# Thirty-two bytes ahead of the arena: every tile of the attention and FFN stages starts on another address

## The reference: what is computed

```
x = even_layer(rms_norm(x)) + x      # sliding-window attention beside an S5 state-space mixer
x = odd_layer(rms_norm(x)) + x       # attention to the 128 keys that an index picks per query
for layer in 0, 1:                   # second block
    h = h + merge_heads(concat(mix, memory)) @ w_out[layer]   # forget-gate attention, then dilated attention
    h = h + conv_ffn(rmsnorm(h))                              # below
return rmsnorm(h, norm_final)

def conv_ffn(xn, w_up, conv_w, conv_b, w_down):
    u = xn @ w_up                    # 512x1024 @ 1024x5632
    c = conv_b + sum(conv_w[j] * shifted(u, j) for j in range(3))
    val, gate = split(c)
    return (silu(gate) * val) @ w_down   # 512x2816 @ 2816x1024
```

## Time and profile before

| | us |
|---|---|
| median of 3 runs | 1809.51 |
| lowest and highest run | 1806.91, 1810.58 |
| the profiled execution's own time | 1806.99 |
| span of its trace | 1805.2 |
| its mean granted TensorE clock | 0.994 of 2.4 GHz |

### The profile page before, as it was taken

One profiled execution on the slowest core, in us unless ns is written; L12 is line 12 of the kernel. 1 busy time (PEld: TensorE's weight loads), 2 busy tenths in 40 slices (PEclk: granted clock), 3 DMA queues, 4 the chain that ended last, 5 costly groups with the idle time before them and its releaser, 6 DMA issues.

```text
span 1805.2 us, 24432 instructions
## 1 busy us (share of the span) xinstructions
PE 1759.5 (97%) x9567; PEld 1404.3 (78%) x9572; DVE 940.4 (52%) x1896; ACT 533.6 (30%) x1183; POOL 1015.1 (56%) x1046
## 2 busy tenths in 40 slices
PE   7999999999989999999999999999999999999998
PEld 6886678676668967779888888887677888888886
DVE  5976754695543355533663166335765356415642
ACT  3614534312542344423220012023664211101111
POOL 7533375554237744335777677756434577677762
PEclk9989999999999999999999999999999999999999
DMA  5220312230233321113332333222111233233331
GB/s 177 82 77 19 117 59 94 77 99 29 71 105 106 94 71 50 69 47 90 106 98 88 95 99 104 88 94 71 49 69 48 70 94 114 96 93 94 95 103 47
DMA packets 170994, 151.16 MB, mean 84 GB/s; under 512 B 5192, under 2 KB 145992, under 8 KB 170880
## 3 DMA queue, kind: packets, MB, share of 16 engines
q1 hardware_dynamic: 169280, 148.12, 26.8%
q10 hardware_dynamic: 1600, 1.48, 0.3%
HBM read 147.45 MB, written 2.14 MB: 83 GB/s over the span
## 4 chain that ended last, share of the span: by engine, by line
PE 93%; DVE 4%; ACT 2%; issue 1%; another core or an unknown queue 0%; DMA 0%; ACTq 0%; DVEq 0%
PE ps L281 77%; PE ps L1989 3%; PE ps L2022 2%; PE ps L2007 2%; PE ps L352 1%; PE ps L640 1%; PE ps L1486 1%; PE ps L1464 1%; PE ps L1995 1%; PE ps L1407 1%; PE ps L1415 1%; PE ps L665 1%; PE ps L1423 0%; PE ps L672 0%; PE ps L1476 0%
## 5 line engine op out<-in xcount | busy, mean ns | idle before, releaser
L127 POOL TENSOR_SCALAR w_hi<-w_raw 128x512 fp32r<-128x512 f32 x520 | 315.7, 635 | 747.0 <-PE ps L281 742.3
L131 POOL TENSOR_TENSOR w_lo<-w_raw,w_hi 128x512 fp32r<-128x512 f32 x520 | 694.5, 1367 | 11.3
L281 PE MATMUL ps<-x_hi,w_hi 128*128 128x512 f32 (+1 forms) x1448 | 538.0, 372 | 0.7 <-DVE x_lo L434 0.7
L281 PE MATMUL ps<-x_hi,w_lo 128*128 128x512 f32 (+1 forms) x1448 | 527.9, 365 | 0.0
L281 PE MATMUL ps<-x_lo,w_hi 128*128 128x512 f32 (+1 forms) x1448 | 527.9, 365 | 0.0
L281 PEld LDWEIGHTS ps<-x_hi,w_hi 128*128 128x128 f32 x1448 | 274.8, 190 | 69.0 <-issue 19.8
L281 PEld LDWEIGHTS ps<-x_hi,w_lo 128*128 128x128 f32 x1448 | 274.8, 190 | 43.7
L281 PEld LDWEIGHTS ps<-x_lo,w_hi 128*128 128x128 f32 x1448 | 275.1, 190 | 40.8 <-issue 0.5
L2291 DVE SCALAR_TENSOR_TENSOR ffn_cv<-ps,col,ffn_cv 128x510 f32<-128x510 f32 (+1 forms) x176 | 131.8, 749 | 192.3 <-ACT ffn_cv L2269 187.6
L2269 ACT ACTIVATE ffn_cv<-ps,col 128x512 f32<-128x512 f32 x88 | 63.8, 775 | 500.2 <-PE ps L281 500.2
L309 DVE TENSOR_TENSOR h<-h,ps 128x512 f32<-128x512 f32 x64 | 43.9, 687 | 261.4 <-PE ps L281 261.3
(11 more groups left out here) (346 smaller groups left out, 2394.1 us busy)
## 6 DMA issues: line engine op xcount, KB each, us to landing
w_raw<-w_up SPq DMA_DIRECT2D x88, 512.0 KB, 5.0
w_raw<-w_down SPq DMA_DIRECT2D x16, 1024.0 KB, 5.0
w_raw<-od_w_in SPq DMA_DIRECT2D x12, 1024.0 KB, 5.2
w_raw<-w_in_fox SPq DMA_DIRECT2D x10, 1024.0 KB, 5.3
w_raw<-w_in_dil SPq DMA_DIRECT2D x10, 1024.0 KB, 5.1
w_raw<-w_out SPq DMA_DIRECT2D x8, 1024.0 KB, 5.0
w_raw<-ev_w_in SPq DMA_DIRECT2D x7, 1024.0 KB, 5.3
w_raw<-w_down SPq DMA_DIRECT2D x8, 768.0 KB, 4.5
```

The source lines that it names most:

```text
L127: ins = pool.tensor_scalar(hi[:, c:min(c + PIECE, size)], raw[:, c:min(c + PIECE, size)], 1.0, 1.0, ALU.mult, ALU.mult)
L131: ins = pool.tensor_tensor(lo[:, c:min(c + PIECE, size)], raw[:, c:min(c + PIECE, size)], hi[:, c:min(c + PIECE, size)].bitcast(F32), ALU. ...
L281: mm = pe.matmul(o, l, r, start=start and i == 0, stop=stop and i == 2)
```

## The change

One tensor of 32 bytes per partition, which nobody reads or writes, is allocated ahead of the arena. The arena's start goes from 133,984 to 134,016, a multiple of 64 bytes (and of 128, as the starts of the weight slots, `h`, `x_hi` and `x_lo` are). Every tile in the arena moves up by 32 bytes. No instruction is added, removed or moved on any engine, and no shape changes; only addresses do.

More of the change, by code:

```diff
@@ L1282, in block_kernel @@
         soft_stat = sb("soft_stat", [P, 4, 4])
+        sb("arena_pad", [P, -nc.sbuf_base % 64 // 4])
         sb("arena", [P, 92 * KB // 4])
```

## The result

The changed kernel takes 1800.82 us, median of 6 runs (1795.70 to 1803.19), against 1809.02 us (1806.91 to 1810.58, 6 runs) for the kernel before: a ratio of 0.9949, with a 95% interval from 0.9931 to 0.9967. That is 8.2 us less. The forecast was 10.6 us less. The profiled execution took 1799.54 us, with a span of 1797.7 us and a mean granted clock of 0.993; before, these were 1806.99 us, 1805.2 us and 0.994.

The account below looks back on a forecast made before the run. TensorE was taken to bound the kernel, through start distances of back-to-back matmuls. 10.1 (back-to-back) + 0.7 (fill) - 0.2 (memory) = 10.6 us off 1,809.51 gave 1,798.9 us, range 1,793 to 1,810 us.

Parts of the forecast that it names:

- The bound: Whole kernel: TensorE bounds, and over each FFN the chain is matmuls alone, so distances between their starts set the time.
- The back-to-back products: 1,527 products of 512 columns with an arena operand, issued without gaps: 6.6 ns less each, 10.1 us gained.
- A line of 64 bytes: Reason given for 6.6 ns per product: an operand starting off a multiple of 64 streams one 64-byte line more.
- The rival of the place: TensorE reads the upper part of a partition more slowly, so nothing changes: 1,809.5 us; 0.20 together with another no-change rival.
- The fill: 201 products between attention steps, worth 1.3 us; half taken, 0.7 us gained, with none to all in the range.
- The memory: 192 products of 256 columns there might get slower once aligned: 0.2 us taken as cost, 0 to 1.0 kept.
- Plain float32, VectorE, ScalarE: Transposes, scores, values and VectorE, ScalarE work: zero taken; reserves up to 5 us gain on transposes, 4.7 us on ScalarE.
- The total: Whole kernel: 10.6 us less, 1,798.9 us; forecast of 1,794 to 1,801 us given a chance of 0.74.

Follow-up runs that it names:

- arena_64_not_128: Changed kernel with a filler of 96 bytes: arena on 134,080, a multiple of 64 but not of 128; 1807.81 us, ratio 1.0000 to the kernel before.
- all_off32: Changed kernel with weights, h, x and arena all moved to 32 bytes past a multiple of 64 (160 modulo 256); 1798.61 us, ratio 0.9947.
- arena_plus160: Changed kernel with a filler of 160 bytes: arena on a multiple of 256, weights and x on 128 modulo 256; 1807.93 us, ratio 0.9999.
- x_off32: Changed kernel with x_hi and x_lo moved to 32 bytes past a multiple of 64, arena on a multiple of 256; 1823.08 us, ratio 1.0081.
- w_lo_off32: Changed kernel with only w_lo moved, to 160 modulo 256, all other operands and the arena on 128; 1822.29 us, ratio 1.0080.
- x_plus160: Changed kernel with x_hi and x_lo begun 160 bytes past the weights' place modulo 256, arena on that place; 1823.23 us in one execution.

## Why the prediction was right, and where it was not

**The bound** was read rightly: the chain of the FFNs shrank by what its products did, and no other engine stepped in.

**The back-to-back products.** 6.6 ns on 1,056 of them in the FFNs makes 7.0 us; the two long pieces gave 3.39 + 3.53 = 6.92 us. The mixers' output projections gave 1.0 us each. The odd output projection gave 0.3 us, where its 72 back-to-back products make 0.5. The step in the earlier trace rows was a sound measure of the gain, since it compared the same instruction with two addresses in one execution.

**The reason given for it was wrong.** "A line of 64 bytes" made the change look necessary and sufficient: any start on a multiple of 64 would do. arena_64_not_128 is on such a start and gains nothing, and all_off32 is on none and gains all. The rows ahead of the prediction showed two groups that differ in the remainder modulo 64, but they differed just as much in whether both operands have the same remainder; the weight slots, x and h are all on 128 modulo 256, so the two could not be told apart. The change happened to fit both, since 134,016 is 128 modulo 256. A filler made by the same rule in another kernel could have landed on 0, 64 or 192 with weights on 128: two of these places, 192 and 0, were run as arena_64_not_128 and arena_plus160, with nothing gained; 64 was run only together with x off place, and the FFN was slow there. That 6.67 ns make 64 bytes of streaming was taken as support for a line of 64 bytes; no run supports such a line, and where the 6.67 ns come from stays open.

**The rival of the place** (0.20) is refuted by the result itself, since the arena became quick where it lies, and by x_off32; the argument against it, that 256 columns showed no step, was a poor one, since those products go the other way (below).

**The fill** was mis-sized. `y` went from 233.1 to 230.7 ns and its stage, 191 to 277 us, gained 0.57 us by the starts, most of it from `att`; the step in between is set by the attention chain. In the two mixers together 2.0 us were gained, where their 312 back-to-back products alone make 2.1: the 72 of fill gave nothing that can be told. Half of 1.3 us should have been nearer to none.

**The memory** cost 0.45 us by the starts (its distance went from 120.3 to 122.6 ns), where 0.2 was taken; inside of 0 to 1.0. The sign is that of two other runs: with `m` off place the distance is 118.6 ns in arena_64_not_128, and that of x with 256 columns is 119.4 ns in x_off32, where x is off place, against 121.6 in the changed kernel. There the same place is the slower one at 256 columns, by 2 to 4 ns; in arena_plus160, w_lo_off32 and x_plus160 by about 1 ns or less.

**Plain float32, VectorE, ScalarE** at zero: `a_L` 279 ns, as before. Of the groups of 16 or more instructions of VectorE and ScalarE, two of `mix_L` moved, by 31 and by 16 ns in opposite directions, and no other by more than 6 ns. For the transposes this says less than it seems. `ident`, at 132,928, begins on a multiple of 64 and not of 128, and in none of these kernels does it share a place modulo 256 with the arena. So their distance, 108.6 to 109.2 ns with `mix_L` and `od_L` everywhere, is measured off place alone. Only `s_cs` (in the place of `h`) with `s_ca` (in the arena) went from two places to one: 274 ns and then 274 ns. The prediction counts 664 transposes; the views have 684 of 128x128, which changes nothing.

**The total.** The addresses give 10.1 us at equal clock, and 9.4 by the starts of the profiled execution, where 10.6 were forecast: the fill and the odd output projection gave less than their terms, and the memory cost more. What missed beyond that is a term the prediction did not have: the clock's stretches at 1.2 GHz, of which the changed kernel gets somewhat more. Over all runs of this study the mean granted clock is 0.9918 in the quick kernels (32 executions) and 0.9932 in those with the arena off place and x on it (83), a difference of 0.0014 with a 95% bound of 0.0007 either way: at 1.55 us per 0.001 some 2 us. The one at 632 us follows a wait of TensorE, and so do those near 182, 440, 499 and 1240 us. But the long one near 92 us doesn't: in both kernels it begins amid small products of the even layer (`head_sum,a_squares`, then `a_u,s_bt`), which follow each other without a wait. That shorter fill makes the stretches more frequent is possible and not shown.

**Loading and streaming.** The trace shows 226.7 ns from start to start at one place and 233.3 at two. The Trainium skill ("TensorE: Matmul & The Clock Gate", section "Step-by-step: what each phase is for") has separate read ports for the moving and the stationary operand, so that loading the next tile takes no read bandwidth from the running product; w_lo_off32 speaks against it, since in the up projections there only the address of one load changes and the product streaming meanwhile takes 9 ns more. By that page the change would have given nothing. The lines of 16 bytes that the Trainium skill gives in "SBUF — State Buffer" (section "SBUF: two separate sides") do not explain it either: every start here is a multiple of 32. That the two reads meet in something which repeats every 256 bytes is what these runs suggest; what it is, they do not show.

## What to carry to other kernels

Where float32r products of 512 columns follow each other without a gap, give all matmul operands in SBUF, moving and stationary, the same start modulo 256 bytes (at 256 columns it cost 2 ns of 120 here), and look at the final addresses, since a small tensor ahead of an arena shifts everything behind it. When a row shows a step between two groups of addresses, list every relation in which they differ, and run the version in which all tiles begin off the suspected alignment together: it separates an absolute alignment from a relative one. For effects under 1% read start distances in the timeline and compare executions at equal granted clock.

## What the runs showed of the hardware that was not expected

- In the down projections of the FFNs, back-to-back float32r products of 512 columns start 226.7 ns apart where the moving tile and the one loaded under it begin on the same place modulo 256 bytes, and 231.7 to 233.3 ns apart otherwise; those of `x` 227.5 ns, and otherwise 233.0 to 234.1. At an offset of -64, tiles of the mixers and `att` show a second rhythm of 229.1 to 229.6 ns.
- At 256 columns it is turned round, and by less: 121.6 to 122.7 ns on the same place; off it 118.6 and 120.3 (the memory in arena_64_not_128 and before) and 119.4 and 120.5 (x in x_off32 and w_lo_off32). The means of the memory's products in x_off32 and w_lo_off32, 129.0 and 128.8 ns, are no effect of addresses: from 544.1 and from 548.6 us on, TensorE is at its 1.2 GHz level for 3.4 us (granted clock 0.50), and 15 and 14 of their distances are 213 or 214 ns. Without these the means are 120.9 and 121.6 ns. In x_off32:

```profile
544.49 0.41 PE L283 MATMUL ps<-m_hi,w_lo 128*128 128x256 f32 x1
544.70 0.41 PE L283 MATMUL ps<-m_hi,w_hi 128*128 128x256 f32 x1
```

- One tile of weights out of three on another place costs as much as three with `x` (233.0 ns), and nearly as much with `ffn_a` (231.7 ns).
- The granted clock falls to 1.2 GHz for pieces of 3.4, 6.8, 10.2 or 13.7 us, outside of the FFNs, at places that differ from one execution to the next. In each of the 13 traces one of them begins between 90 and 97 us, amid small products that follow each other without a wait. The executions of the kernel before lie between 1801.87 and 1813.97 us (53), those of the changed one between 1795.70 and 1805.69 us (24); what the clock leaves unexplained of this spread has a standard deviation of 1.2 us.
